# A row ring of seven places and contiguous partial sums in the value phase of a PEER expert mixer

## The reference, cut to what matters

```
s = einsum('bhpd,hpkd->bhpk', q, sub_keys);  sv, si = top_k(s, 16)
... idx = i1 * 128 + i2,  gate = softmax(cv)      # 128 experts per token
act = gelu(einsum('bhkd,bd->bhk', u_emb[idx], xb))
out = einsum('bhk,bhkd->bd', gate * act, v_emb[idx])
```

## Time and profile before

| what | value |
|---|---|
| median of 3 runs | 2043.56 us (2042.26 to 2045.56) |
| profiled execution | 2031.1 us from the first to the last instruction; its own time outside that span is not listed |
| TensorE matmul / weight load busy | 95% / 86% |
| VectorE / ScalarE / GpSimd busy | 72% / 37% / 40% |
| HBM traffic | 221 GB/s over the span |
| value phase, first matmul to last | 1405.6 to 2017.6 us |

### The profile page before, as it was taken

The page is one execution under the profiler, slowest core; times in us unless marked ns, Lnnn a source line. Parts: engine busy times, 40 slices in busy tenths (PEclk is TensorE's granted clock), DMA queues, the critical chain, the costliest instruction groups (busy, mean ns, idle before and its releaser), DMA issues.

```text
span 2031.1 us, 35532 instructions
## 1 busy us (share of the span) xinstructions
PE 1929.3 (95%) x14267; PEld 1754.1 (86%) x14267; DVE 1461.1 (72%) x2696; ACT 754.0 (37%) x953; POOL 810.6 (40%) x600
## 2 busy tenths in 40 slices
PE   8998977888999999999999999999999999999996
PEld 8998966676469999988888888888999999999995
DVE  6526564775257788878887897886787687778786
ACT  6334543442132224345445444543332232232232
POOL 8244737650023101322422331221688455555551
PEclk9999988999999999999999999999999999999998
DMA  6212210021222136777987887789999999999984
GB/s 202 64 56 65 64 40 2 9 91 52 83 87 84 43 140 216 260 267 269 365 316 280 305 327 286 276 285 380 390 340 358 348 325 347 358 323 353 357 309 145
DMA packets 179179, 450.11 MB, mean 222 GB/s; under 512 B 15728, under 2 KB 92272, under 8 KB 168816
## 3 DMA queue, kind: packets, MB, share of 16 engines
q1 hardware_dynamic: 125472, 240.77, 34.4%
q0 software_dynamic: 42496, 151.03, 20.5%
q10 hardware_dynamic: 11088, 56.63, 6.8%
HBM read 383.26 MB, written 65.07 MB: 221 GB/s over the span
## 4 chain that ended last, share of the span: by engine, by line
PE 51%; DVE 18%; DMA 17%; issue 9%; ACT 4%; POOL 2%; SPq 0%; ACTq 0%; DVEq 0%; POOLq 0%
PE bank L1935 23%; DMA rows_v<-in_pv,pick 11%; PE bank L1352 6%; PE bank L1889 5%; PE bank L1841 3%; DVE xs L2835 3%; DMA rows_v<-in_pv,gate 3%; DVE w_lo L2853 3%; PE bank L1944 2%; DMA sca<-in_pu_rows,pick 2%; PE bank L1372 1%; PE bank L1911 1%; DVE u_lo L2594 1%; DVE sca L2600 1%; DVE mixT L2835 1%
## 5 line engine op out<-in xcount | busy, mean ns | idle before, releaser
L834 POOL DMA_INDIRECT sca<-in_pu_rows,pick x128 | 174.1, 1360 | 527.1 <-DVE sdot L2600 413.0
L1935 PE MATMUL bank<-xhi,u_hi 128*128 128x448 f32 x1008 | 379.0, 376 | 1.2 <-ACT actb L1228 1.2
L2020 PE MATMUL bank<-w_hi,v_hi 128*128 128x416 f32 x1024 | 362.1, 354 | 14.5 <-DVE w_lo L2853 13.7
L1935 PE MATMUL bank<-xhi,u_lo 128*128 128x448 f32 x1008 | 368.9, 366 | 0.0
L1935 PE MATMUL bank<-xlo,u_hi 128*128 128x448 f32 x1008 | 368.0, 365 | 0.0
L2020 PE MATMUL bank<-w_lo,v_hi 128*128 128x416 f32 x1024 | 359.0, 351 | 0.0
L2020 PE MATMUL bank<-w_hi,v_lo 128*128 128x416 f32 x1024 | 359.0, 351 | 0.0
L834 POOL DMA_INDIRECT rows_v<-in_pv,pick x128 | 242.3, 1893 | 195.5 <-DVE xs L2835 134.5
L1281 ACT ACTIVATE v_hi<-v_raw 128x4096 fp32r<-128x4096 f32 x32 | 116.2, 3633 | 380.3 <-DMA v_raw<-in_pv 380.3
L2835 DVE SCALAR_TENSOR_TENSOR xs<-rows_v,sdot,xs 128x1024 f32<-128x1024 f32 x127 | 162.9, 1283 | 103.2 <-DMA rows_v<-in_pv,pick 97.3
L2020 PEld LDWEIGHTS bank<-w_hi,v_hi 128*128 128x128 f32 x1024 | 192.6, 188 | 24.0 <-DVE w_lo L2853 21.9
(11 more groups left out here) (694 smaller groups left out, 3587.1 us busy)
## 6 DMA issues: line engine op xcount, KB each, us to landing
u_raw<-in_pu SPq DMA_DIRECT2D x64, 1024.0 KB
v_raw<-in_pv SPq DMA_DIRECT2D x128, 512.0 KB
act_scratch<-actb ACTq DMA_DIRECT2D x64, 448.0 KB
wts<-act_scratch SPq DMA_DIRECT2D x32, 896.0 KB
gate_scratch<-gst ACTq DMA_DIRECT2D x13, 2048.0 KB
gring<-gate_scratch SPq DMA_DIRECT2D x32, 832.0 KB
wring<-in_w_q SPq DMA_DIRECT2D x4, 2048.0 KB, 9.0
wp_raw<-in_w_in SPq DMA_DIRECT2D x7, 1024.0 KB, 5.4
```

Source lines behind the costliest of these rows:

```text
L834: pool.indirect_dma_start(dst, None, rows[:, :], bass.IndirectOffsetOnAxis(at, 0)).then_inc(s_row[s % RING], 16)
L1935: ins = mm(bank[b][:, 0:DS], lhsT, rhs[:, 0:DS], **on)
L2020: ins = mm(bank[c][:, 0:VD], lhsT, rhs[q][:, e, 0:VD], **on)
```

## The change

The ring for value rows has seven places instead of four. Four lie where they lay; three (`rows_x`) lie where `mixT` was. The partial sums of the 32 other tokens move to a block of their own, `few_t`, contiguous, also in the memory of `mixT`. `few_t` and `rows_x` take 16 KB of its 18 KB per partition. The u-phase keeps its ring of four. Three more semaphores are wanted, and to make room for them `m_ready` is joined to `tails_ready`, `iota_ready` to `constants_ready`, and the two slot counters (`u_slot_seen`, `v_slot_seen`) become one.

```
--- before.py
+++ after.py
@@ -57,6 +57,7 @@
 S_FIRST = 48
 ADD_ORDER = [("s", i) for i in range(S_FIRST)] + [("e", i) for i in range(XV)] + [("s", i) for i in range(S_FIRST, SLOTS)]
 RING = 4
+VRING = 7
 GSC = 32768.0
 GC = 32
 NCH = DS // GC
@@ -104,6 +105,10 @@
         mix_sc = ExitStack()
         mixT = sb("mixT", [128, KD, NT], scope=mix_sc)
         mix_sc.close()
+        sums_sc = ExitStack()
+        few_t = sb("few_t", [128, KD, 128], scope=sums_sc)
+        rows_x = sb("rows_x", [128, VRING - 4, D], scope=sums_sc)
+        sums_sc.close()
         xlo = sb("xlo", [128, KD, NT], f32r)
         mixers = ExitStack()
 
@@ -277,7 +282,7 @@
         few_pick, few_at = [gate[:, 3, XV * i:XV * i + XV].bitcast(u32) for i in range(2)]
         few_gate, few_sel = [gate[:, 3, XV * i:XV * i + XV] for i in range(2, 4)]
         few_act, few_w = [gate[:, 0, XV * i:XV * i + XV] for i in range(2)]
-        few_sum = acc[:, :, DS:NT]
+        few_sum = few_t[:, :, :]
         first = ExitStack()
         w_out_sc = ExitStack()
         w_o = sb("w_o", [128, 2, KD, 512], scope=w_out_sc)
@@ -343,7 +348,7 @@
         rows_u = [sca[:, 1 + r // 2, D * (r % 2):D * (r % 2) + D] for r in range(RING)]
         second = ExitStack()
         v_lo1 = sb("v_lo1", [128, GE * D], f32r, scope=second)
-        rows_v = sb("rows_v", [128, RING, D], scope=second)
+        rows_v = sb("rows_v", [128, 4, D], scope=second)
         w_hi1 = sb("w_hi1", [128, GE, DS], f32r, scope=second)
         sb("gap2", [128, 256], scope=second)
         v_lo0 = sb("v_lo0", [128, GE * D], f32r, scope=second)
@@ -359,6 +364,7 @@
         sb("gap5", [128, 512], scope=second)
         v_raw0 = sb("v_raw0", [128, GE * D], scope=second)
         v_hi0 = sb("v_hi0", [128, GE * D], f32r, scope=second)
+        v_rows = [rows_v[:, r, :] for r in range(4)] + [rows_x[:, r, :] for r in range(VRING - 4)]
         v_raw, v_hi, v_lo = [v_raw0, v_raw1], [v_hi0, v_hi1], [v_lo0, v_lo1]
         wts, gring, w_hi, w_lo = [wts0, wts1], [gring0, gring1], [w_hi0, w_hi1], [w_lo0, w_lo1]
         x1_late = [v_raw0[:, D * t:D * t + D] for t in range(4)] + [v_raw1[:, 0:D]]
@@ -392,6 +398,7 @@
         s_grp = [sem("group_loaded0"), sem("group_loaded1")]
         s_row = [sem(f"row_gathered{r}") for r in range(RING)]
         s_few = sem("few_acts_gathered")
+        s_vrow = s_row + [sem(f"value_row_gathered{r}") for r in range(RING, VRING)]
 
         c_dve, c_act, c_pool = sem("vector_step"), sem("scalar_step"), sem("gpsimd_step")
         s_const = sem("constants_ready")
@@ -515,9 +522,9 @@
             sp.wait_ge(s_pj, LAST[6] + 1)
             load_narrow(0)
             load_narrow(1)
-            sp.wait_ge(S("m_ready"), 1)
+            sp.wait_ge(S("tails_ready"), 1)
             sp.dma_start(m_o, mo[:, :]).then_inc(s_out, 16)
-            sp.wait_ge(S("tails_ready"), 1)
+            sp.wait_ge(S("tails_ready"), 2)
             sp.dma_start(conv_o, conv_t[:, :, :, :]).then_inc(s_tail, 16)
             for h in range(MLH):
                 for j in range(4 * h + 2, 4 * h + 4):
@@ -535,7 +542,7 @@
             sp.wait_ge(s_init, 16 * 8)
             for dst, src in [(s0[:, :, :, :], s0_d), (g2[:, :], g2_d)]:
                 sp.dma_start(dst, src).then_inc(s_init, 16)
-            sp.wait_ge(S("tails_ready"), 2)
+            sp.wait_ge(S("tails_ready"), 3)
             sp.dma_start(shift_o, shift_t[:, :, :]).then_inc(s_tail, 16)
             for p in range(4):
                 if p == 2:
@@ -578,7 +585,7 @@
             with sp.Fori(0, UG // 2 - 1) as i:
                 for q in range(2):
                     sp.wait_ge(S(f"u_lo_ready{q}"), i + 1)
-                    sp.sem_inc(S("u_slot_seen"), 1)
+                    sp.sem_inc(S("slot_seen"), 1)
                     sp.dma_start(u_raw[:, q, :, :], pu[bass.ds(i * 2 + (2 + q), 1)].squeeze(0)).then_inc(s_u[q], 16)
 
             pv_g = pv.rearrange("(g e p) d -> g p e d", e=GE, p=128)
@@ -625,7 +632,7 @@
 
                     sp.wait_ge(S("w_lo_ready"), i * 2 + (q + 1))
                     sp.wait_ge(S("v_lo_ready"), i * 2 + (q + 1))
-                    sp.sem_inc(S("v_slot_seen"), 1)
+                    sp.sem_inc(S("slot_seen"), 1)
                     g = bass.ds(i * 2 + (2 + q), 1)
                     load_acts(q, act_d[g].squeeze(0))
                     sp.wait_ge(S("sum_done"), i * 16 + 8 * (q + 1) + 5)
@@ -821,22 +828,19 @@
                 prep(p)
             pool.wait_ge(S("mix_ready"), 8)
             pool.iota(io128[:, :], pattern=[[1, 128]], base=0, channel_multiplier=0,
-                      allow_small_or_imprecise_dtypes=True).then_inc(S("iota_ready"), 1)
-            pool.wait_ge(S("iota_ready"), 1)
+                      allow_small_or_imprecise_dtypes=True).then_inc(s_const, 1)
+            pool.wait_ge(s_const, 3)
             for j in range(16):
                 pool.wait_ge(s_high, HIGH[f"q{j}"])
                 ring, cs = j // 4 % 2, query_cols(j)
                 TT(wring_lo[:, ring, :, cs], wring[:, ring, :, cs], wq_hi[j % 4].bitcast(f32), ALU.subtract).then_inc(s_low, 1)
 
-            def gather(s, dst, rows, used, at):
-                if s >= RING:
-                    pool.wait_ge(S(used), s - RING + 1)
-                pool.indirect_dma_start(dst, None, rows[:, :], bass.IndirectOffsetOnAxis(at, 0)
-                                        ).then_inc(s_row[s % RING], 16)
-
             pool.wait_ge(S("picked"), 1)
             for s in range(SLOTS):
-                gather(s, rows_u[s % RING], pu_rows, "row_used", pick[:, s:s + 1])
+                if s >= RING:
+                    pool.wait_ge(S("row_used"), s - RING + 1)
+                pool.indirect_dma_start(rows_u[s % RING], None, pu_rows[:, :], bass.IndirectOffsetOnAxis(pick[:, s:s + 1], 0)
+                                        ).then_inc(s_row[s % RING], 16)
 
             pool.wait_ge(S("row_used"), SLOTS)
             pool.wait_ge(S("dots_done"), 2 * GU + GU * UG)
@@ -848,7 +852,11 @@
                 if 16 <= s < 16 + XV:
                     pool.indirect_dma_start(few_act[:, s - 16:s - 15], None, act_flat,
                                             bass.IndirectOffsetOnAxis(few_at[:, s - 16:s - 15], 0)).then_inc(s_few, 16)
-                gather(s, rows_v[:, s % RING, :], pv, "row_added", pick[:, i:i + 1] if kind == "s" else few_pick[:, i:i + 1])
+                at = pick[:, i:i + 1] if kind == "s" else few_pick[:, i:i + 1]
+                if s >= VRING:
+                    pool.wait_ge(S("row_added"), s - VRING + 1)
+                pool.indirect_dma_start(v_rows[s % VRING], None, pv[:, :], bass.IndirectOffsetOnAxis(at, 0)
+                                        ).then_inc(s_vrow[s % VRING], 16)
 
 
         @block.scalar
@@ -2140,7 +2148,7 @@
                 last = TT(v[0], v[1], v[2][:, :, w - 1:w].to_broadcast([4, (hi - lo) // w, w]), ALU.add)
             last.then_inc(S("rows_ready"), 1)
             link(dve.tensor_copy(mo[:, 0:1], r["m"][:, SEQ - 1:SEQ]))
-            dve.tensor_copy(mo[:, 1:], r["m"][:, SEQ + NS - 1:NT:NS]).then_inc(S("m_ready"), 1)
+            dve.tensor_copy(mo[:, 1:], r["m"][:, SEQ + NS - 1:NT:NS]).then_inc(S("tails_ready"), 1)
             def conv(h):
                 done = {}
                 for j in range(CW):
@@ -2558,7 +2566,7 @@
             for t in range(3, 5):
                 columns_low(t)
 
-            dve.wait_ge(S("iota_ready"), 1)
+            dve.wait_ge(s_const, 3)
             link(dve.tensor_copy(lane16[:, :, :], io128[:, 0:16].unsqueeze(2).to_broadcast([128, 16, 2])))
 
             tmps = [sc2[:, 0:128], sc2[:, 128:256], sc3[:, 0:128]]
@@ -2825,11 +2833,11 @@
                 kind, i = ADD_ORDER[s]
                 total = accS[:, :].rearrange("p (c d) -> p c d", c=KD) if kind == "s" else few_sum
                 weight = sdot[:, i:i + 1] if kind == "s" else few_w[:, i:i + 1]
-                row = rows_v[:, s % RING, :].rearrange("p (c d) -> p c d", c=KD)
+                row = v_rows[s % VRING].rearrange("p (c d) -> p c d", c=KD)
                 if kind == "e" and i == 0:
                     dve.wait_ge(s_few, 16 * XV)
                     link(TT(few_w, few_act, few_gate, ALU.mult))
-                dve.wait_ge(s_row[s % RING], 16 * ((SLOTS + s) // RING + 1))
+                dve.wait_ge(s_vrow[s % VRING], 16 * (s // VRING + 1 + (SLOTS // RING if s % VRING < RING else 0)))
                 if i:
                     dve.wait_ge(S("row_added"), s)
                     ins = STT(out=total, in0=row, scalar=weight, in1=total, op0=ALU.mult, op1=ALU.add)
```

10 lines of the change are left out of this document (5 added, 5 removed).

## The result

The changed kernel takes 2016.89 us (median of 4 runs, 2014.95 to 2018.81), the kernel before 2044.56 (4 runs, 2042.26 to 2045.74): a ratio of 0.9879, interval 0.9846 to 0.9911, 27.7 us less. The interval excludes no change; the gain is 1.2%. Forecast were 2017.9 us and 25.7 less. In two later series the ratio was 0.9823 (0.9776 to 0.987) and 0.986 (0.9829 to 0.9891).

A forecast was written before the change was run, and what follows sets the result against it. A loop through VectorE's adds and a late row gather was taken to set the pace. 21.9 - 3 (DMA) - 2 (first fill) + 6.4 (tail) + 2.4 (clock) = 25.7 us less: 2017.9 us, range 2011 to 2024 (chance 0.57).

The forecast's parts named there:

- The loop: Value phase: v_lo, w_lo, add, gather, add take 18.96 us against TensorE's 18.05; cutting it removes 21.9 us of waits.
- The DMA engines: Value phase: share rises from 94.7% to 98.4% at 357 GB/s, leaving 3 us of the 21.9 (bounds 0 and 8).
- Rival A: DMA engines become the bound and TensorE waits for v_raw instead of rows; 2031 us, chance 0.27.
- B: Rival: nothing gained, v_raw takes over the whole wait and the last row the tail; 2043 us, chance 0.08.
- C: Rival: slower, v_raw lands later in every group and SyncE's loads set the pace; 2059 us, chance 0.08.
- the second loop: SyncE's loads, started from w_lo, through v_raw, v_hi, v_lo, w_lo: 29.9 us for two groups of 36.1, slack 6.2.
- the prediction's own sign of being wrong: v_raw landing over 26 us after the group in work began, or GpSimd still late with rows.
- First fill: Start of value phase: three more gathers at once delay the third group, costing nothing to 2.1 us, once; 2 taken.
- Tail: End of value phase: the last adds end sooner, so the transposes wait less; gain 6.4 us (bounds 4.0 and 7.5).
- Clock: Behind the tail's stall TensorE ran at its 1.2 GHz level; without the stall 2.4 us gained (bounds 0 and 2.4).
- Edits at nothing: Contiguous few_t, rows_x under mixT and the joined semaphores neither cost nor gain time.
- The base: Median of runs, 2043.56 us, lies 12.5 us above the profiled span of 2031.1, taken as fixed.

The follow-up runs named there:

- the weights put into it: Kernel before, ring of four, with v_lo and w_lo of the next group ahead of a group's first two adds on VectorE: 2124.0 us, ratio 1.0377.
- the hold: Changed kernel, ring of seven, but only four gathers let out ahead of the adds until gather 16: 2005.89 us, in a second series 2009.19.
- the block: Kernel before with its ring of four, only the partial sums of the other tokens moved to contiguous few_t: 2046.47 us, ratio 0.9979.
- its second profile: Changed kernel run once more with no edit, beside the kernel before: 2012.08 us.

## Why the prediction was right, point by point

- **The loop.** Right. With one place more it is cut (pace 17.92, nothing but the third group waits), and with the weights put into it the time grows by about what the loop's sum says. The 21.9 us all went; the third group's 5.8 are new.
- **The DMA engines.** 3 us were set aside, none was lost. Share 97.6% at 360 GB/s. Rival A falls, and so do B and C: the second loop, that of SyncE's loads, holds TensorE up at the third group alone. There the prediction's own sign of being wrong did show, v_raw landed over 26 us after the group in work began (31.5).
- **First fill.** The step that was mis-sized: "between nothing and 2.1 us", "I take 2", where the first profile has 5.8 us of wait and 2.3 at the lower clock behind it, the hold gives back 8 us of the phase, and 5 to 6 by the medians. It priced three rows by their bytes at 406 GB/s, so v_raw was to land up to 3.9 us later; it landed 7.2 us later. It left out that beside small packets a row takes nearly the whole rate, so that the gates were late and v_raw behind them. (Four rows more, not three, are asked for in the first 21 us: 12 gathers against 8 in the two first profiles. The fifth of the later ones goes out at 20.4 us after the first matmul, when the gates are late already.) It also had no term for a fall of the clock there. The Trainium skill (DMA: Bandwidth & Descriptors, Queues, rings and completion order) has the turns go by packets; the prediction weighed that rule by bytes, at half the rate each. The trace agrees with turns by packet: 382 to 417, with 1.40 to 0.22 MB. Whether the profile's packets, which have 4 KB and less, are the page's, which hold several descriptors each, no run here shows.
- **Tail.** 6.4 us forecast, wait 7.5 to 0.3: 7.2. w_lo ran far enough ahead that the last add, done at 1982.2 us, was no longer in the way of the transposes at 1992.15. The prediction had this as its upper bound.
- **Clock.** 2.4 forecast for the tail. From the first transpose to the end it was 2031.1 - 2006.29 = 24.8 us and is 2014.5 - 1992.15 = 22.4: 2.4. Not foreseen was that the first fill would cause a fall of its own.
- **Edits at nothing.** Right for the block (0.9979, 1284 ns). The joined semaphores weren't run alone.
- **The sum.** From the first matmul of the phase to the end the two first profiles differ by (2031.1 - 1405.6) - (2014.5 - 1415.3) = 26.3 us, forecast 25.7. Terms of both signs made up for each other: first fill 6 worse, DMA 3 better, tail 0.8 better, and a pace of 186.7 instead of 188 ns, worth 4 us, which the same code doesn't always have (188.3 in its second profile); about 1 us is not assigned. That the terms cancel so well is luck. So is the start: the two first profiles differ by 16.6 us in their spans, as the later one began its phase 9.7 us later.
- **The base.** "12.5 us above, taken as fixed" was wrong. 1.7 us lie outside; the other 11 were the distance of a short execution from the median. The working by differences held all the same: 2043.56 - 25.7 uses the median alone, and the 12.5 cancel. A pair of like executions (the kernel before and the changed one, once more each) gives 2037.6 - 2013.6 = 24.0 us; their waits give 22.9 - 6.2 for w_lo, 7.6 - 0.5 in the tail, 2.4 of clock there, and -2.3 for the clock at the third group: 23.9. That it meets 24.0 to 0.1 us is luck too. The sum leaves out two short falls of the clock in that execution of the kernel before (1.6 us lost in each), and its phase began 0.9 us earlier.

What stays open: why the phase starts between 1405.6 and 1416.5 us from one execution to the next, what sets the pace to one of its two values, and why the gates of the third group get past six rows (12.4 us) but not past seven (19.0 to 20.2). Six places were profiled once.

**The better version.** Seven places with the hold until gather 16, or simply five: 2006 to 2009 us, 5 to 6 less than the changed kernel in the same series by the medians. Five need 4 KB per partition for the added places instead of 12.

## What to carry to other kernels

When a prefetched transfer shows up in the chain, write the loop down piece by piece, queues included: which instruction frees the place, what stands between it and the use. Its sum against the pace of the bounding engine tells how many places are wanted (here one, not three), and it also tells what a reordering will do. A deeper ring can have a price at its first fill: here it was 8 us with seven places and little with five. Take no more places than the loop wants, or start at the old depth and let the ring grow once the loads beside it have got through.

## What the runs showed of the hardware that was not expected

- The DMA engines took the gathers' queue and the hardware queue packet for packet (382 to 417 in 4 us), so the queue with packets of 3.7 KB got 1.40 MB and the one with packets of 0.5 KB got 0.22. Beside v_raw it was 235 to 239, with 0.83 and 0.85 MB.
- One kernel's pace at the higher clock was 186.7 ns a matmul in one execution and 188.3 in another, worth 5 us in this phase. It changed at a stop of TensorE, in either direction, and held in the 520 us without a stop behind it.
- A stop of TensorE of 5.8 us in the midst of steady work brought the granted clock to 0.50, and cost 2.3 us more; the many stops of up to 3.2 us before left no such mark in the first profile. In the second profile of the kernel before, two stops of 2.6 and 2.2 us did: the granted clock was 0.57 from 1693 to 1697 us and 0.59 from 1882 to 1885. So the length of a stop alone doesn't tell.
